# Mixer jobs of layer 0 in another order, all convolution taps on VectorE

## The reference

```python
h = rms_norm(x, norm_w)
q, k, v, iq, ik, iw, glu_in = split(h @ w_in)          # 1024,128,128,1024,64,16,2048 columns
q = rms_norm(q by head); k = rms_norm(k)               # 8 heads of 128, one k/v head
score = sum_h relu(iq_h @ ik.T) * iw_h                 # 16 indexer heads of 64, causal
sel = top_k(score, 64)                                 # 64 keys for each query
attn = softmax(q @ k_sel.T * scale + rel_bias) @ v_sel
a, g = split(glu_in)                                   # 1024 channels each
u = a * sigmoid(g)
u = causal depthwise conv of u, 31 taps, + bias
conv = silu(layer_norm(u) * ln_g + ln_b)
x = x + concat(attn, conv) @ w_out
```

## Time and profile before

| | |
|---|---|
| time, median of 3 runs | 1806.95 us (1803.94 to 1807.29) |
| span of the profiled execution | 1802.9 us |
| TensorE busy | 1667.0 us (92%) |
| VectorE busy | 1467.3 us (81%) |
| ScalarE busy | 1128.2 us (63%) |
| POOL busy | 271.0 us (15%) |
| first product of `kvi` | 26.85 us |
| first product of `wa0` | 328.8 us |
| last tap done | 401.9 us |
| first product of `wc0` | 421.9 us |

### The profile page before, as it was taken

How to read it: one execution, slowest core, us unless ns; L and a number is a source line. 1 busy time by engine, 2 the same in 40 slices (tenths; PEclk the granted TensorE clock), 3 DMA queues, 4 the chain that set the end, 5 groups by cost and what they waited for, 6 DMA issues and landing times.

```text
span 1802.9 us, 23197 instructions
## 1 busy us (share of the span) xinstructions
PE 1667.0 (92%) x8093; PEld 1381.7 (77%) x8093; DVE 1467.3 (81%) x1521; ACT 1128.2 (63%) x1351; POOL 271.0 (15%) x257
## 2 busy tenths in 40 slices
PE   5999878877789999999999998789999999999998
PEld 5998668656668887887887886678887887887886
DVE  3235899996559989989988996769989989998996
ACT  3334325645348877777777775347777777777784
POOL 0000799770000011003003000000002003002000
PEclk7699989998789999999999998889999999999999
DMA  9334433334359979988997996239988988997992
GB/s 310 130 131 139 140 117 116 106 107 142 115 182 376 380 280 346 378 310 306 373 383 248 383 348 232 93 112 370 373 312 317 376 333 297 376 381 261 362 374 90
DMA packets 99919, 473.43 MB, mean 263 GB/s; under 512 B 18506, under 2 KB 21852, under 8 KB 49668
## 3 DMA queue, kind: packets, MB, share of 16 engines
q1 hardware_dynamic: 93508, 465.59, 69.8%
q10 hardware_dynamic: 6336, 6.88, 1.2%
HBM read 470.32 MB, written 2.11 MB: 262 GB/s over the span
## 4 chain that ended last, share of the span: by engine, by line
PE 66%; DVE 20%; issue 8%; ACT 4%; DMA 1%; ACTq 1%; POOL 1%; DVEq 0%; POOLq 0%
PE ps L1461 20%; PE ps L1463 20%; PE ps L1462 20%; DVE split_lo L966 9%; DVE work L1002 5%; PE ps L1720 2%; DVE cat L966 2%; DVE xn L962 1%; ACT split_hi L618 1%; PE ps L1701 1%; PE ps L1427 1%; PE ps L1562 1%; ACT xn L626 1%; ACT cat L618 1%; ACTq L445 0%
## 5 line engine op out<-in xcount | busy, mean ns | idle before, releaser
L966 DVE TENSOR_TENSOR split_lo<-ring,split_hi 128x1024 fp32r<-128x1024 f32 (+1 forms) x880 | 1115.1, 1288 | 223.3 <-ACT split_hi L618 177.2
L618 ACT ACTIVATE split_hi<-ring 128x1024 fp32r<-128x1024 f32 (+1 forms) x880 | 924.5, 1059 | 308.4 <-PE ps L1463 289.6
L1461 PE MATMUL ps<-split_hi,cat 128*128 128x512 f32 (+2 forms) x1824 | 733.6, 402 | 56.9 <-DVE split_lo L966 39.9
L1462 PE MATMUL ps<-split_lo,cat 128*128 128x512 f32 (+2 forms) x1824 | 718.0, 394 | 0.0
L1463 PE MATMUL ps<-split_hi,cat 128*128 128x512 f32 (+2 forms) x1824 | 718.0, 394 | 0.0
L1461 PEld LDWEIGHTS ps<-split_hi,cat 128*128 128x128 f32 x1824 | 354.8, 195 | 166.4 <-DVE split_lo L966 63.2
L1463 PEld LDWEIGHTS ps<-split_hi,cat 128*128 128x128 f32 x1824 | 354.9, 195 | 71.9
L1462 PEld LDWEIGHTS ps<-split_lo,cat 128*128 128x128 f32 x1824 | 355.4, 195 | 65.4
L606 POOL TENSOR_TENSOR x_sb<-work,x_sb 128x512 f32<-128x512 f32 x48 | 81.2, 1692 | 943.2 <-ACT work L618 943.2
L1461 PE MATMUL ps<-cat,split_hi 128*128 128x256 f32 x384 | 115.0, 300 | 13.5 <-DVE split_lo L966 13.3
L1462 PE MATMUL ps<-cat,split_hi 128*128 128x256 f32 x384 | 111.2, 290 | 0.0
(11 more groups left out here) (159 smaller groups left out, 787.0 us busy)
## 6 DMA issues: line engine op xcount, KB each, us to landing
ring<-in_w_gate SPq DMA_DIRECT2D x128, 1024.0 KB, 5.7
ring<-in_w_up SPq DMA_DIRECT2D x128, 1024.0 KB, 5.7
ring<-in_w_down SPq DMA_DIRECT2D x128, 1024.0 KB, 5.7
ring<-in_w_in_e SPq DMA_DIRECT2D x32, 1024.0 KB, 5.1
ring<-in_w_out_e SPq DMA_DIRECT2D x16, 1024.0 KB, 5.1
ring<-in_pool_w_o SPq DMA_DIRECT2D x4, 1024.0 KB, 7.9
x_sb<-in_x SPq DMA_DIRECT2D x2, 1024.0 KB, 7.1
ring<-in_w_in_e SPq DMA_DIRECT2D x8, 256.0 KB, 6.1
```

The lines of the kernel that those rows point to most:

```text
L618: return nc.scalar.activation(out, in_, ACT.Copy, scale=scale)
L966: return tt(dst, full, hi.bitcast(F32), ALU.subtract)
L1461: mm(out, sh, mh, start=start, stop=False, **how)
L1462: mm(out, sh, ml, start=False, stop=False, **how)
```

## The change

- The nine projection jobs run in the order `a0, g0, kvi, iq0, iq1, a1, g1, q0, q1`.
- `kvi` has one product of 336 columns where it had one of 256 and one of 80: 12 a half.
- The bias flip is cut in two, `flip0` and `flip1`, both beside `kvi`; the indexer jobs are beside `a1` and `g1`; the turning of q, the logits, the turning of the probabilities and the attention come after `q1`, with no products between them.
- All 248 taps are on VectorE, in groups of 2, 3 or 6 after splits and in groups of 2, 8 and 20 between steps of the attention. POOL and ScalarE have none.
- The small loads are issued after four blocks instead of eight. Banks are assigned anew, and `bias_up` lies in `iqT`.

```diff
-    jobs = [("kvi", (0, 1)), ("iq0", (4, 5)), ("kT", (6,)), ("iq1", (0, 1)), ("flip", (2, 3, 4, 5))]
+    jobs = [("a0", (0, 1)), ("g0", (4, 5)), ("flip0", (2, 3)), ("flip1", (2, 3)), ("kvi", (6, 7)), ("iq0", (4, 5)), ("kT", (0,)),
+            ("iq1", (2, 3))]
...
-        DVE_CHUNKS = ((0, 1), (4, 5))
-        POOL_CHUNKS, SHARED_CHUNKS = (3, 2), (6, 7)
+        CHUNK_PAIRS = ((0, 1), (2, 3), (4, 5), (6, 7))
+        CONV_TAPS = CC * TAPS
...
-                if b == RING:
+                if b == RING // 2:
                     small_loads()
...
+            def convolve(more):
+
+                end = min(at[1] + more, taps_open[0])
+                for n in range(at[1], end):
...
+            split_past("g0", 3)
+            dve.wait_ge(vec_out, 1)
+            gated_input(0)
+            split_past("kvi", 3, 2)
...
-            split_past("iq0", 7)
+            split_past("iq1", 3, 3)
...
-                split_past("g0", r)
-                if r == 2:
-                    gated_input(0)
+                split_past("g1", r)
+                if r == 4:
+                    gated_input(1)
...
+            dve.wait_ge(bias_out, 2)
...
-            split_past("q1", 2, 3)
+            split_past("q1", 0, 3)
             normalise_q(1)
-            split_past("q1", 7, 3)
+            split_past("q1", 2, 2)
...
             for t in range(NT):
-                split_past("a1", 2 + 2 * t, 2)
+                convolve(8)
                 dve.wait_ge(exp_done, t + 1)
                 nc.vector.reciprocal(srec[:, t, :], ssum[:, t, :]).then_inc(prob_step, 1)
-            split_past("g1", 2, 3)
+            convolve(20)
+            split_past("q1", 4, 2)
...
             for n in range(3):
-                split_past(f"wa{n}", 2, 4)
+                split_past(f"wa{n}", 2, 6)
                 add_job(f"wa{n}")
-            split_past("wa3", 0, 4)
-
-
-            convolve(at[1], DVE_TAPS)
+            split_past("wa3", 0, 6)
+            convolve(CONV_TAPS)
...
-            def kvi_job():
+            def kvi_job(between):
 
                 start_job("kvi")
                 for q in range(8):
-                    if q == 4:
-                        turn_vectors()
-                    kv = next_unit(2, KVW)
-                    ki = unit(q % SPLITS, 2, IKW, 2 * KVW)
+                    between(q)
+                    w = next_unit(2, KVW + IKW)
                     for k in range(2):
-                        first, end = q == 0 and k == 0, q == 7 and k == 1
-                        for t in range(NT):
...
+                        for t, b in enumerate(BANKS["kvi"]):
+                            last = product(ps[:, b, 0:KVW + IKW], pick_parts(hT, ALL, 2 * q + k, slice(t * P, (t + 1) * P)),
+                                           pick_parts(w, ALL, k), q == 0 and k == 0, q == 7 and k == 1)
...
+            channels_job("a0", beside_a0)
+            channels_job("g0")
+            kvi_job(beside_kvi)
             channels_job("iq0", beside_iq0)
-            channels_job("iq1", beside_iq1)
-            channels_job("a0", beside_a0)
-            channels_job("g0", beside_g0)
+            channels_job("iq1")
+            channels_job("a1", beside_a1)
+            channels_job("g1", beside_g1)
             tokens_job("q0")
             tokens_job("q1")
-            channels_job("a1", beside_a1)
-            channels_job("g1", beside_g1)
+            for i in range(4):
+                turn_q(i)
+            for t in range(NT):
+                logits(t)
+            for i in range(6):
+                turn_probs(i)
```

More of the change, by code:

```diff
@@ L94 @@
 BANKS = dict(JOBS)
-STREAM = [(name, 4) for name in ("kvi", "iq0", "iq1", "a0", "g0", "q0", "q1", "a1", "g1")]
-STREAM += [(f"wa{n}", 2) for n in range(4)] + [(f"wc{n}", 2) for n in range(4)]
-STREAM_END = {name: sum(2 * k for _, k in STREAM[:i + 1]) for i, (name, _) in enumerate(STREAM)}
+STREAM = [(name, 8) for name in ("a0", "g0", "kvi", "iq0", "iq1", "a1", "g1", "q0", "q1")]
+STREAM += [(f"wa{n}", 4) for n in range(4)] + [(f"wc{n}", 4) for n in range(4)]
+STREAM_END = {name: sum(k for _, k in STREAM[:i + 1]) for i, (name, _) in enumerate(STREAM)}
 def job_number(name):
@@ L376, in parts @@
                     rows = slice(4 * kq + 2 * h, 4 * kq + 2 * h + 2)
-                    mid, end = h * HALF + 2 * KVW, h * HALF + 2 * (KVW + IKW)
-                    out.append((ring[:, slot, h * HALF:mid].rearrange("p (k n) -> p k n", k=2), w_in[:, rows, K0:K0 + KVW]))
-                    out.append((ring[:, slot, mid:end].rearrange("p (k n) -> p k n", k=2), w_in[:, rows, IK0:IK0 + IKW]))
+                    both = ring[:, slot, h * HALF:h * HALF + 2 * (KVW + IKW)].rearrange("p (k n) -> p k n", k=2)
+                    out.append((both[:, :, 0:KVW], w_in[:, rows, K0:K0 + KVW]))
+                    out.append((both[:, :, KVW:KVW + IKW], w_in[:, rows, IK0:IK0 + IKW]))
                 return out
@@ L394, in build @@
         POOL0 = NMIX + ROUND
-        kvi_at = range(4)
+        kvi_at = range(8, 12)
         def mixer_landed(b):
@@ L584, in _ @@
                     head_root(1 + NT * i + t, hrs[:, t, heads], hms[:, t, heads], hsq[:, t, heads], 4)
[L585 to L592, removed]
             pool.wait_ge(ln_step, 4)
@@ L671, in _ @@
             act.dma_start(bias_dram, bias_row).then_inc(bias_stored, 16)
[L673 to L678, removed]
-            for t in range(NT):
-                sq = nc.scalar.activation(il_relu[:, t, 0:P], ps[:, t, 0:P], ACT.Square, accum_out=ksq[:, t:t + 1])
-            sq.then_inc(kvi_out, 1)
-            split_past("kvi", 4)
+            split_past("a0", 4)
             act.wait_ge(bias_stored, 16)
@@ L696, in iq_copy @@
                      ps[:, first:first + 2, :].rearrange("p b n -> p (b n)")).then_inc(iq_out, 1)
-            split_past("iq0", 1)
+            split_past("iq0", 2)
             iq_copy(0)
[L700 to L703, removed]
+            split_past("iq1", 2)
             iq_copy(1)
             for i in range(12):
-                split_past("iq1", 3 + i)
+                split_past("iq1", 4 + i)
                 wait_job(f"il{i}")
@@ L710, in _ @@
                 nc.scalar.activation(il_relu[:, i % 2, :], ps[:, BANKS[f"il{i}"][0], :], ACT.Relu).then_inc(relu_done, 1)
[L712 to L719, removed]
+            split_past("g1", 3)
+            gate_tanh(1)
             def q_squares(i):
@@ L724, in q_squares, with q_out @@
                 for t in range(NT):
[L725 to L734, removed]
+                    nc.scalar.activation(qn[:, t, 512 * i:512 * i + 512], ps[:, BANKS[f"q{i}"][t], :], ACT.Square).then_inc(qsq_done, 1)
+            def q_out(i):
                 t, hq = i // 2, i % 2
@@ L765, in _ @@
                      ps[:, BANKS[f"oT{i}"][0], :].rearrange("p (h s) -> p h s", h=4)).then_inc(oT_out, 1)
[L766 to L778, removed]
             split_past("wa3", 0)
@@ L988, in _ @@
             split_channels()
-            conv_ops = [(chunks[i], w) for chunks in DVE_CHUNKS for w in range(TAPS) for i in range(2)]
-            def convolve(first, last):
-                for n in range(first, last):
+            conv_ops = [(chunks[i], w) for chunks in CHUNK_PAIRS for w in range(TAPS) for i in range(2)]
+            at = [0, 0]
+            taps_open = [0]
+            def convolve(more):
+                end = min(at[1] + more, taps_open[0])
+                for n in range(at[1], end):
                     c, w = conv_ops[n]
@@ L1014, in split_to @@
                         .then_inc(mixer_lo, 1)
-                    more = min(taps, taps_open[0] - at[1])
-                    convolve(at[1], at[1] + more)
-                    at[1] += more
+                    convolve(taps)
                 at[0] = end
```

172 lines of the change are left out of this document (74 added, 98 removed).

## The result

The changed kernel takes 1764.73 us (median of 4 runs, 1761.41 to 1766.52), the kernel before 1807.12 in the same session (1803.94 to 1807.77). The ratio is 0.9765, 95% interval 0.9751 to 0.9779: 2.35% faster. Forecast were 1769, 1754 to 1790, and faster with 0.91. The profiled execution has a span of 1759.6 us against 1802.9, 43.3 us less.

What follows compares the result with a forecast made beforehand. TensorE was taken as busy most of the span, with VectorE busy and TensorE idling from 185.0 us while POOL convolves. 0.4 - 39.5 - 2.5 = -41.6, less 4 for stalls, gave -37.6: 1769 us, range 1754 to 1790.

Steps and rivals of the forecast that it cites:

- attention chain: From the end of `q1` to `wa0`, with no products as cover: 42 us, bounds 34 and 50.
- `wa0` to the last tap: VectorE sets the pace with splits, six taps each, additions and 49 left-over taps: 70.6 us, where it took 73.1.
- tail to `wc0`: The stretch after the last tap, 401.9 to 421.9 in the kernel before: untouched, 20 us.
- stalls at job borders: Allowance for small waits between the projection jobs: 4 us, turning -41.6 into -37.6.
- the clock rises under the work of `a0`: First job: one half at 5.1 us, seven at 2.88; rival that it stays at 1.2 GHz: 1803 us, chance 0.05.
- The 0.153 us for 336 columns: Price taken for one `kvi` product, between 0.12 and 0.23 by width; 96 products take 14.7 us.
- The price of a tap: On VectorE in the convolution: 0.88 us beside a working POOL, 0.40 alone, so 248 taps take 99 us.
- 0.48 in groups: Rival on VectorE: a tap alone costs 0.08 us more when it stands in groups; 1784 us, chance 0.05.
- 0.88 throughout: Rival on VectorE: slow taps are not POOL's doing, so 248 taps cost 0.88 us each; 1864 us, chance 0.03.
- the group of a split and three taps: Between steps of the old attention chain: 4.07 us each, now gone; against the rival of 1807 us, chance 0.05.
- The reciprocal stands behind 16 taps: In the attention chain on VectorE: 6.4 us of taps before the reciprocal, which brings the chain to 25.5 us.
- The half clock: TensorE in the attention chain partly at half rate: 42 us, against 37 at full clock and 45 at half throughout.

Runs made afterwards that it cites:

- the merged job: The kernel before, order kept, with only `kvi` changed to products of 336 columns instead of 256 and 80 apart: 1783.09 us, ratio 0.9861.
- the narrow one: The changed kernel with `kvi` cut into products of 256 and 80 columns again, in its new third place: 1771.1 us, ratio 0.9794.
- without the early taps: The changed kernel without the 64 taps beside `kvi`, `iq0` and `iq1`, which are done at the end instead: 1785.45 us, ratio 0.9893.

## Why the prediction was right

Term by term, forecast and measured:

| term | forecast | measured |
|---|---|---|
| `a0` and `g0` | 50.0 | 49.6 |
| `kvi` | 18.3 | 18.2 |
| `iq0` to `g1` | 108.0 | 107.7 |
| `q0`, `q1` | 44.2 | 44.3 |
| attention chain | 42 | 39.7 |
| `wa0` to the last tap | 70.6 | 69.3 |
| tail to `wc0` | 20 | 21.8 |
| stalls at job borders | 4 | 0 |
| change of the span | -37.6 | -43.3 |

**The clock.** The step that the clock rises under the work of `a0`, 256 columns for every weight load, held, and two experiments carry it: the merged job rose in the old place, and the narrow one stayed up in the new. The 0.153 us for 336 columns held as well: a `kvi` half without a flip took 1.84 to 1.85 us.

**The price of a tap.** It was read from one chain, 0.88 beside POOL and 0.40 alone; the rivals that doubted it (0.48 in groups, 0.88 throughout) were refuted by the 2.38 us for six, and POOL as the cause was shown by giving POOL work again. One reading was too general: the 0.88 holds beside POOL's additions of the shared chunks. Beside its other work has 0.79 (three taps in 2.38 us), and the group of a split and three taps that the prediction puts at 4.07 us is 3.89 in the rows shown and comes to 4.07 further on. No term of the sum rests on this, only the rivals.

**The chain.** Its length was sized well, but not for the reasons in every step. ScalarE alone would have taken nearly as long through the middle: the exponentials end at 269.46, the first scaling follows at once and ends at 271.89, and the second begins at 272.01. The chain of waits goes through the 16 taps there, but the second reciprocal, behind them, is ready at 271.98, only 0.1 us after ScalarE. That step of the working, "The reciprocal stands behind 16 taps", cost next to nothing; all 44 taps together cost the chain about 1.1 us. The half clock was there: the mean of the window is 0.70, with the two sets of logits at 6.80 us in one row. How much of it a run meets varies: the same logits took 5.53 us in the kernel with taps beside the indexer jobs.

**What was mis-sized.** The allowance of 4 us for stalls was not needed: TensorE has no pause of note before `q1` ends. The tail is 1.8 us longer, and the prediction called it untouched. TensorE now waits 18.7 us for the last taps where it had waited 0.9, and its channel sum runs at a mean clock of 0.56. From the tail of the kernel before:

```profile
401.95 2.01 PE ps L1607 x8
...
408.86 4.63 DVE split_lo L966 x4
```

The channel sum takes 3.50 us instead of 2.01, which is 1.5 of the 1.8. The sum of squares takes 6.92 instead of 4.9, but before, the tail did not wait for it: four splits on VectorE ended later, at 413.49 against 411.73, so that only 0.3 us of its 2 are new. The span came out 5.7 us under the forecast: 4 of the allowance, 2.3 of the chain, 1.3 of the `wa` stage and 0.7 of the jobs, less 1.8 of the tail and 0.7 of the start and of what lies behind `wc0`.

**Where the gain comes from.** The merged product alone gives 24.0 us, all taps on VectorE alone gives nothing, and without the early taps the changed kernel's 42.4 us fall by 20.7. (Singly these need not add up, since each part was taken from or put to another whole.) By these runs the move of the taps pays where an input of the convolution is ready ahead of stretches that TensorE bounds, and this order makes it so by putting `a0` and `g0` first. The chain without cover cost less than the pauses of TensorE that it replaces: TensorE is idle 17.8 us in it, and was idle 26.3 us in 185.0 to 328.8.

Two things stay open. Whether the chain could again lie beside products in the new order was not tried. Neither was the new order with POOL and ScalarE keeping their share of the taps, so what the move of the taps is worth inside the new order is argued, from the two prices of a tap and the kernel without early taps, and not measured by itself.

## What to carry to other kernels

Work for an engine that sets the pace costs its full price, and the same work costs nothing beside another engine's stretch as long as it fits there: 36 taps were worth 14.7 us at the end and nothing beside the indexer jobs, where VectorE was then busy 50.5 of 61.2 us. So find out where the first inputs can be ready early before moving work to it. Two engines that share the load of a loop may not add up: compare the price of one instruction with its neighbour busy and silent, in one chain. And a matrix engine that is 100% busy can still be at half clock: look at the granted clock of the first job. Here one product where there had been two brought it up.

## What the runs showed of the hardware

- The same products ran at either level of the clock: 256 and 80 columns in turn for 43.8 us at 0.50 after a pause of 4.5 us, and for 25.4 us at 1.00 right behind a job at full clock. With 336 columns, after the same pause, the clock was at 1.00 within 7.2 us.
- What POOL does sets how much it slows VectorE: an fp32 tap of two SBUF inputs took 0.40 us alone, 0.75 beside POOL multiplying a tile by itself, 0.79 to 0.84 beside POOL multiplying and adding in turn, and 0.88 beside POOL's additions one behind the other; a split took 1.13, 1.55, mostly 1.49 to 1.63, and 1.66 to 1.68.
- The Trainium skill ("Vector Engine (DVE) Microarchitecture Reference", Points that are easy to get wrong) says that such an operation with two non-bf16 SBUF sources halves throughput. Read as half of one element a cycle, with the clock of 0.96 GHz in "VectorE: DVE Perf Modes" (Specifications), six taps would take 3.2 us, an estimate. The trace disagrees: six took 2.38 us.
